# Four-layer sequence mixer on one NeuronCore: the gate tiles and the latent norm of layer 0, and the head norms of layer 3, laid out another way

## The chip, the cores and the metric

The kernel runs on one core of a Trainium2 chip. The metric is the device time of one execution in microseconds (us). The engines are named as in the profile: PE is TensorE (matmul), PEld its weight loads, DVE is VectorE, ACT is ScalarE, POOL is GpSimd, SP is SyncE.

## What is computed

The input is `x`, 256 tokens by 2048 features in fp32. Four layers follow one another: latent attention (layer 0), mLSTM (layer 1), HGRN2 (layer 2) and an attention with forget bias (layer 3). The change touches layers 0 and 3 alone. Of the reference, cut to what matters:

```python
def _mla_mixer(x, cos, sin, w_in, q_norm, w_qb, kv_norm, w_kvb, w_out):        # layer 0
    proj = x @ w_in                                                             # 512 + 512 + 64 + 2048 columns
    c_q, c_kv, k_rope, z = jnp.split(
        proj, [Q_LORA, Q_LORA + KV_LORA, Q_LORA + KV_LORA + QK_ROPE], axis=-1)
    q = (_rmsnorm(c_q, q_norm) @ w_qb).reshape(b, s, MLA_HEADS, MLA_QK)
    kv = (_rmsnorm(c_kv, kv_norm) @ w_kvb).reshape(b, s, MLA_HEADS, QK_NOPE + V_HEAD)
    ...
    attn = _chunk_causal_attention(q, k, v).reshape(b, s, MLA_WIDTH)
    return (attn * jax.nn.silu(z)) @ w_out

def head_rmsnorm(x, w):                                                         # layer 3: keys, queries, outputs
    xf = x.astype(jnp.float32)
    return xf * lax.rsqrt(jnp.mean(xf * xf, axis=-1, keepdims=True) + EPS) * w.astype(jnp.float32)
```

In layer 3 keys, queries and attention outputs are each normed per head (16 heads of 128).

## The kernel before

**The stream of products.** All projections are one stream of units through the three engines. A unit is two 128-row blocks of a weight matrix by up to 512 columns. SP loads it to `wraw` (8 buffers). ACT rounds it to fp32r (`high`, L249), DVE forms the rest `wraw - whi` (`low`, L257), and PE multiplies (`products`, L287 to L289: `x_hi*w_hi`, `x_hi*w_lo`, `x_lo*w_hi` for two row blocks and two token halves, 12 matmuls). `whi` and `wlo` have 4 buffers (`SPLIT`), so that ACT may be 4 units ahead of PE: `high` of unit n waits until PE is done with unit n-4 (`w_used`), `low` waits for `high`, and PE for `low`. A tile of the output is 16 row blocks (8 units) where the input is the layer's, 4 row blocks (2 units) where it is the latents'. `evac` copies a finished tile out of PSUM, the first token half on ACT (L329, in layer 3 L988) and the second on DVE (L335, L1596), in the step three units (`LAG`) behind its last unit.

**The order of side work.** Each engine's program is written out by hand as a loop over p, the units of a phase: first the stream's own part of unit p, then side work that hangs on certain values of p. An engine does its instructions in order, so that a side step that waits holds up the stream's next unit on that engine.

**Layer 0.** The phases are `l0_in` (tiles c_q, c_kv, and a narrow one of 64 columns for the rotary key: 24 units), `l0_0` to `l0_3`, and `l0_out` (32 units). Phase `l0_s` holds some gate tiles z (512 columns of `w_in`, 8 units each) and then four small tiles, 2 units each: queries (384 columns) and keys and values (512 columns) of two head pairs. `Z_FIRST` says which gate tiles a phase holds. Its products are followed one phase later by the attention of its four heads, in 11 stages (`l0_side`), which PE does after unit `i * nu // 11` of a phase of nu units (`spread`), and ACT and DVE three units later:

```python
        Z_FIRST = [0, 2, 3, 4, 4]
...
        def l0_at(name):
            return spread(L0_STAGES, 12 if name == "l0_out" else length(name))
```

So `l0_0` has 24 units, `l0_1` and `l0_2` 16, and `l0_3` 8. A group's stages begin with the rotation of the queries (`rope`, L1671 to L1674 on DVE) and the gate's exponentials (`z_exp`, L1045 to L1047 on ACT); then PE transposes queries and keys (`pair`, L2393 to L2396), and the scores, softmax (L562), transposes (L571), values (L587 to L589) of four heads follow; last `back` turns the group's output (L381 on PE, L394 on ACT, L409 on DVE) for `l0_out`, whose first unit waits for the third group's.

**The latent norm** stands between `l0_in` and the small tiles of `l0_0`. ACT squares the two latents for both token halves with a running sum (`latents`, four ACTIVATEs on L1017, after unit 4 of `l0_0`), DVE makes the mean (L1686), ACT takes `Ln` and `Exp` (L978, L979), DVE scales the latents (`latents2`, L1695), PE turns them (`latents2`, four groups of four transposes on L381, after unit 7), and each of the four groups then goes DVE (L403, times the weight column) to ACT (L394) to DVE (L409) to become `tb_hi` and `tb_lo` (`latents3`, all four in one piece after unit 10). The key's rotary part takes its way through PE, DVE, PE and ACT between them (L2357, L1679 to L1684, L2364, L1028).

**Layer 3.** `l3_kv` and `l3_q` have four groups of four heads, 16 units each. Three things are normed in a group: the keys at step 3 of the next `l3_kv` group (`kv_side`), the queries at step 11 of their own (`q_side` `norm`), and the outputs in step 9 of the next `l3_q` group (`post`). Each norm is this: ACT takes eight Squares with accumulator output, one for each head and token half, every one waiting for the one before (L1376 for keys and queries, L1440 for outputs); DVE scales the eight sums (L2206); ACT takes `Ln` and `Exp` (L1381, L1383); DVE multiplies (L2209, twice). DVE is in `head_norm` from the L2206 on, and ACT in `inverse_root`.

Of the kernel before, what the change touches and what calls it, by code (L numbers as in the profile page):

```python
# [84 lines left out]
def build(nc, a, out):  # L85

    with ExitStack() as ctx:
# [125 lines left out]
        Z_FIRST = [0, 2, 3, 4, 4]  # L213
# [595 lines left out]
        sqj = A(P)  # L809
# [3 lines left out]
        l3 = sems(3, "r_dg r_row f_row f_e f_ok ksq kv_ krs kn kt kT qsq qv qrs qn qt qT sc msk mx ex pt ptc pv o "  # L813
# [148 lines left out]
        def _(act):  # L962
# [37 lines left out]
            first_step("l0_in", TA, False)  # L1000
            for p in range(SPLIT, length("l0_in")):
                step(act, high, evac, "l0_in", p)
                if p == 12 + LAG:
                    act.wait_ge(rope_arg, 2)
                    nc.scalar.activation(sin.rearrange("p a b -> p (a b)"), angle[:, 4, :], ACT.Sin).then_inc(rope_ok, 1)
                    nc.scalar.activation(cos.rearrange("p a b -> p (a b)"), angle[:, 5, :], ACT.Sin).then_inc(rope_ok, 1)

                    nc.scalar.add_instruction(mybir.InstLoadActFuncSet(
                        name=nc.get_next_instruction_name(), engine=mybir.EngineType.Activation,
                        act_func_set_id=LN_EXP_SET, ins=[], outs=[]))  # L1010

# [14 lines left out]
            def latents3():  # L1026
                act.wait_ge(l0["kr_pe"], 1)
                nc.scalar.activation(krT, ps[:, 0, 0:T], ACT.Copy).then_inc(l0["kr_T"], 1)  # L1028
                for j in range(2):
                    for b in range(TB):  # L1030
                        turn_act(act, turn, TBf[0][:, 4 * j:4 * j + 4, b * P:(b + 1) * P], True)
# [337 lines left out]
            def squares(pre, src, g):  # L1369

                for b in range(TB):
# [13 lines left out]
            def kv_side(g, p):  # L1385
                def norm():
                    landed(act, "l3_kv", 0, g)
                    squares("k", qw3, g)
                    inverse_root(l3["kv_"], l3["krs"], g)
# [29 lines left out]
            def q_side(g, u):  # L1419
                c = 4 * g  # L1420

                def norm():
                    landed(act, "l3_q", 0, g)
                    squares("q", qw3, g)
# [7 lines left out]
                def post():  # L1432
# [3 lines left out]
                    for b in range(TB):  # L1436
                        for h in range(4):
                            if b or h:
                                act.wait_ge(l3["sq"], 8 * g + 4 * b + h)
                            nc.scalar.activation(sqj, o3[:, b, h * HD:(h + 1) * HD], ACT.Square,  # L1440
                                                 accum_out=sm[:, 32 + 4 * b + h:33 + 4 * b + h]).then_inc(l3["sq"], 1)
# [62 lines left out]
        def _(dve):  # L1504
# [171 lines left out]
            def latents():  # L1676
# [20 lines left out]
            def latents3():  # L1697
                for j in range(2):
                    for b in range(TB):
                        d = (slice(4 * j, 4 * j + 4), slice(b * P, (b + 1) * P))  # L1700
                        turn_dve(dve, turn, TBf[0][:, d[0], d[1]], TBf[1][:, d[0], d[1]], colA[:, 4 * j:4 * j + 4])
# [501 lines left out]
            def head_norm(dst, src, sq, vs, rs, on, g):  # L2203

                dve.wait_ge(sq, 8 * g + 8)
# [14 lines left out]
            def kv_side(g, p):  # L2220
                if p == late("l3_kv", 0):
                    head_norm(qw3, qw3, l3["ksq"], l3["kv_"], l3["krs"], l3["kn"], g)
# [20 lines left out]
            def q_side(g, u):  # L2243

                def norm():
                    head_norm(qw3, qw3, l3["qsq"], l3["qv"], l3["qrs"], l3["qn"], g)
# [12 lines left out]
                def post():  # L2259
                    head_norm(o3, o3, l3["sq"], l3["v"], l3["rs"], l3["on"], g)  # L2260
# [63 lines left out]
        def _(pe):  # L2324
# [28 lines left out]
            def key_part():  # L2353
                landed(pe, "l0_in", 2)
                pe.wait_ge(col_ok, 3)
                for b in range(TB):
# [477 lines left out]
```

## Time and profile before

| | |
|---|---|
| median of 3 runs | 1892.11 us (1891.86 to 1893.95) |
| the profiled execution | 1891.89 us |
| its span in the trace | 1890.10 us |
| PE busy, share of the span | 1856.6 us, 98% |
| DVE busy | 1241.5 us, 66% |
| ACT busy | 982.9 us, 52% |
| DMA: mean rate over the span | 169 GB/s, 319.28 MB |

The profiled execution's own time is 1.8 us above its span, which is what lies around the trace, and it lies 0.2 us below the median. A PE that is busy for 98% isn't one at its peak: the ends of matmuls are modelled (a row has 0.39 us where the next matmul starts 0.23 us after it), so that idle time in a row of PE understates the time lost by about 0.16 us each. The start of one row minus the start of the row before it gives the loss without that.

### The profile page before, as it was taken

How to read it: one execution, taken by the hardware profiler on the slowest of the kernel's cores; microseconds unless marked ns; L12 is line 12 of the kernel's file. 1: busy time of each engine (PE TensorE's matmuls, PEld its weight loads, DVE VectorE, ACT ScalarE, POOL GpSimd, SP SyncE). 2: the span in 40 equal slices, each digit the busy share in tenths (PEclk: the TensorE clock that was granted, in tenths of full speed). 3: DMA queues.
4: the chain of work that ended last, by engine and by line, in shares of the span. 5: the costliest groups of instructions: out<-in, count | busy, mean ns of one | idle time of the engine just before them, and what ended most of it. 6: DMA issues, size and time to landing. Idle time of an engine off the chain costs nothing.

```text
span 1890.1 us, 25046 instructions
## 1 busy us (share of the span) xinstructions
PE 1856.6 (98%) x9049; PEld 1559.8 (83%) x9049; DVE 1241.5 (66%) x1672; ACT 982.9 (52%) x1516; POOL 27.6 (1%) x106
## 2 busy tenths in 40 slices
PE   8999989999999999999999999999999999999999
PEld 7888878878888888887888888888878888878787
DVE  6566665687557755658777777777766555566664
ACT  4455564355456545536554454544435455566652
POOL 4000000000000000000000000000000000000000
PEclk9999999999999999999999999999999999999999
DMA  6665434468789877565545454544456566545453
GB/s 233 210 187 149 145 117 135 145 206 184 182 164 201 183 184 168 200 237 156 161 160 157 144 167 144 164 147 156 146 166 204 179 189 191 164 142 161 146 170 116
DMA packets 170207, 319.28 MB, mean 169 GB/s; under 512 B 16601, under 2 KB 20849, under 8 KB 169345
## 3 DMA queue, kind: packets, MB, share of 16 engines
q1 hardware_dynamic: 168992, 313.70, 56.7%
q10 hardware_dynamic: 576, 4.19, 0.5%
q8 instruction: 60, 0.98, 0.2%
q0 software_dynamic: 544, 0.13, 0.0%
q14 instruction: 35, 0.28, 0.0%
HBM read 315.88 MB, written 2.10 MB: 168 GB/s over the span
## 4 chain that ended last, share of the span: by engine, by line
PE 45%; DVE 2%; ACT 2%; issue 2%; ACTq 0%; DVEq 0%
PE acc L287 13%; PE acc L289 13%; PE acc L288 13%; PE ps L2640 3%; PE ps L538 1%; ACT whi L249 1%; DVE wlo L257 1%; PE ps L2624 0%; DVE arena L2014 0%; PE ps L381 0%; ACT arena L1440 0%; ACT arena L1376 0%; PE ps L2614 0%; PE ps L571 0%; PE ps L2721 0%
## 5 line engine op out<-in xcount | busy, mean ns | idle before, releaser
L257 DVE TENSOR_TENSOR wlo<-wraw,whi 128x1024 fp32r<-128x1024 f32 (+3 forms) x616 | 713.7, 1178 | 412.6 <-ACT whi L249 409.8
L249 ACT ACTIVATE whi<-wraw 128x1024 fp32r<-128x1024 f32 (+3 forms) x616 | 615.0, 1017 | 340.2 <-PE acc L289 334.4
L287 PE MATMUL acc<-whi,ta_hi 128*128 128x512 f32 x1664 | 659.4, 396 | 2.5 <-DVE wlo L257 2.3
L289 PE MATMUL acc<-whi,ta_lo 128*128 128x512 f32 x1664 | 648.6, 390 | 0.0
L288 PE MATMUL acc<-wlo,ta_hi 128*128 128x512 f32 x1664 | 647.9, 389 | 0.0
L287 PEld LDWEIGHTS acc<-whi,ta_hi 128*128 128x128 f32 x1664 | 312.6, 188 | 68.1 <-issue 3.4
L289 PEld LDWEIGHTS acc<-whi,ta_lo 128*128 128x128 f32 x1664 | 312.3, 188 | 66.6
L288 PEld LDWEIGHTS acc<-wlo,ta_hi 128*128 128x128 f32 x1664 | 312.8, 188 | 61.8
L287 PE MATMUL acc<-whi,tb_hi 128*128 128x512 f32 (+1 forms) x704 | 278.6, 396 | 8.2 <-DVE wlo L257 6.5
L289 PE MATMUL acc<-whi,tb_lo 128*128 128x512 f32 (+1 forms) x704 | 271.9, 386 | 0.0
L288 PE MATMUL acc<-wlo,tb_hi 128*128 128x512 f32 (+1 forms) x704 | 271.7, 386 | 0.0
L287 PEld LDWEIGHTS acc<-whi,tb_hi 128*128 128x128 f32 x704 | 132.7, 189 | 34.7 <-DVE wlo L257 9.1
L289 PEld LDWEIGHTS acc<-whi,tb_lo 128*128 128x128 f32 x704 | 132.7, 189 | 26.0
L288 PEld LDWEIGHTS acc<-wlo,tb_hi 128*128 128x128 f32 x704 | 132.9, 189 | 23.4
L1304 ACT ACTIVATE arena<-arena 128x512 f32<-128x512 f32 x64 | 37.4, 634 | 122.0 <-DVE arena L2034 122.0
L2640 PEld LDWEIGHTS ps<-arena 128*128 128x128 f32 x448 | 54.3, 191 | 2.1
L2640 PE MATMUL ps<-arena 128*128 128x64 f32 x448 | 53.0, 271 | 0.0
L562 ACT ACTIVATE arena<-arena,sm 128x128 f32<-128x128 f32 x64 | 28.7, 449 | 45.5 <-DVE sm L552 44.6
L329 ACT ACTIVATE arena<-acc 128x512 f32<-128x512 f32 (+3 forms) x41 | 22.5, 549 | 44.9 <-PE acc L289 42.8
L2034 DVE TENSOR_TENSOR arena<-arena 128x1024 f32<-128x1024 f32 x32 | 38.4, 1210 | 0.0
L381 PE MATMUL ps<-ident,x_res 128*128 128x128 f32 x160 | 25.8, 314 | 11.7 <-DMA x_res<-in_x 6.0
L538 PE MATMUL ps<-arena 128*128 128x128 f32 (+1 forms) x192 | 36.8, 331 | 0.0
(312 smaller groups left out, 1324.3 us busy)
## 6 DMA issues: line engine op xcount, KB each, us to landing
wraw<-in_ml_w_in SPq DMA_DIRECT2D x128, 512.0 KB, 6.1
wraw<-in_a_w_in SPq DMA_DIRECT2D x128, 512.0 KB, 4.0
wraw<-in_kv_w SPq DMA_DIRECT2D x64, 512.0 KB, 3.8
wraw<-in_b_w_in SPq DMA_DIRECT2D x64, 512.0 KB, 4.3
wraw<-in_mla_w_in SPq DMA_DIRECT2D x48, 512.0 KB, 5.3
wraw<-in_mla_w_out SPq DMA_DIRECT2D x32, 512.0 KB, 3.7
wraw<-in_ml_w_out SPq DMA_DIRECT2D x32, 512.0 KB, 4.6
wraw<-in_a_w_out SPq DMA_DIRECT2D x32, 512.0 KB, 4.4
```

The source lines that it names most:

```text
L249: nc.scalar.activation(whi[:, n % SPLIT, :, 0:w], wraw[:, n % RAW, :, 0:w], ACT.Copy).then_inc(w_high, 1)
L257: nc.vector.tensor_tensor(wlo[:, n % SPLIT, :, 0:w], wraw[:, n % RAW, :, 0:w], whi[:, n % SPLIT, :, 0:w].bitcast(F32), ALU.subtract).then_ ...
L287: nc.tensor.matmul(o, xh, wh, start=first, stop=False)
L288: nc.tensor.matmul(o, xh, wl, start=False, stop=False)
L289: m = nc.tensor.matmul(o, xl, wh, start=False, stop=end)
L329: nc.scalar.activation(dst, result(name, k, 0, dst.shape[0]), ACT.Copy).then_inc(out_b0, 1)
L381: m = nc.tensor.transpose(ps[:, c % 4, j * P:(j + 1) * P], s, ident[:])
L538: m = nc.tensor.matmul(o, x, y, start=i == 0, stop=i == len(parts) - 1)
L562: nc.scalar.activation(v, v, ACT.Exp, bias=sm[:, 2 * w + b:2 * w + b + 1], accum_out=sm[:, 4 + 2 * w + b:5 + 2 * w + b]).then_inc(self.l[" ...
L1304: nc.scalar.activation(d[:, :, c, :], d[:, :, c, :], ACT.Exp, scale=(-1.0, 1.0)[c]).then_inc(l2["ee"], 1)
L2034: nc.vector.tensor_tensor(dT[:, j % 2, :].rearrange("p (n r) -> p n r", r=2 * h), b, b[:, :, h - 1:h].to_broadcast([P, G4 // (2 * h), 2 * h]),
L2640: m = nc.tensor.matmul(ps[:, 2 + j % 2, n * 64:(n + 1) * 64], k[:, h, b * P:(b + 1) * P], qx[:, j % 2, n * 64:(n + 1) * 64], start=True, s ...
```

## The change

It has three parts.

1. `Z_FIRST` becomes `[0, 1, 2, 3, 4]`. Each of the phases `l0_0` to `l0_3` now holds one gate tile and 16 units, and the stages of each group spread over 16.
2. The latent norm begins in `l0_in`: the Squares stand after unit 20 (a narrow one) on ACT, the mean after `low` of unit 21 on DVE, `Ln` and `Exp` after unit 22 on ACT, the scaling after unit 0 of `l0_0` on DVE, PE's transposes after unit 1, and the four turned groups one by one after units 2, 3, 4 and 5 on ACT and DVE. The key's rotary part comes after them. PE's wait for all turned latents stands ahead of unit 8, the first of a small tile.
3. In layer 3 the eight accumulating Squares of a norm become one ACTIVATE of 128x1024 elements that writes the squares to two PSUM banks, and DVE sums them per head with one `tensor_reduce`, eight sums of 128 elements, ahead of its scaling.

```diff
-        Z_FIRST = [0, 2, 3, 4, 4]
+        Z_FIRST = [0, 1, 2, 3, 4]
...
+                if p == 20:
+                    latents()
+                if p == 22:
+                    latents2()
+
+            def latents3(i):
+                j, b = i // 2, i % 2
+                turn_act(act, turn, TBf[0][:, 4 * j:4 * j + 4, b * P:(b + 1) * P], True)
...
                 step(act, high, evac, "l0_0", p, 0, ("l0_in", 0))
-                if p == 4:
-                    latents()
-                if p == 6:
-                    latents2()
+                if 2 <= p < 6:
+                    latents3(p - 2)
                 if p == 10:
-                    latents3()
+                    key_part()
...
-            def squares(pre, src, g):
-
-                for b in range(TB):
-                    for h in range(4):
-                        n = 8 * g + 4 * b + h
-                        if b or h:
-                            act.wait_ge(l3[pre + "sq"], n)
-                        nc.scalar.activation(sqj, src[:, b, h * HD:(h + 1) * HD], ACT.Square,
-                                             accum_out=sm[:, 32 + 4 * b + h:33 + 4 * b + h]).then_inc(l3[pre + "sq"], 1)
+            def squares(done, src):
+
+                nc.scalar.activation(ps2(2), src.rearrange("p b n -> p (b n)"), ACT.Square).then_inc(done, 1)
...
+                if p == 21:
+                    dve.wait_ge(l0["lat_sq"], 4)
+                    nc.vector.tensor_scalar(sm[:, SMALL + 4:SMALL + 8], sm[:, SMALL:SMALL + 4], 1.0 / LORA, EPS,
+                                            ALU.mult, ALU.add).then_inc(l0["lat_v"], 1)
...
                 step(dve, low, evac, "l0_0", p, 0, ("l0_in", 0))
-                if p == 4:
-                    latents()
-                if p == 6:
+                if p == 0:
                     latents2()
-                if p == 10:
-                    latents3()
+                if 2 <= p < 6:
+                    latents3(p - 2)
+                if p == 7:
+                    key_part()
...
-            def head_norm(dst, src, sq, vs, rs, on, g):
-
-                dve.wait_ge(sq, 8 * g + 8)
+            def head_norm(dst, src, sq, ss, vs, rs, on, g):
+
+                dve.wait_ge(sq, g + 1)
+                nc.vector.tensor_reduce(sm[:, 32:40], ps2(2).rearrange("p (n d) -> p n d", d=HD), AX,
+                                        ALU.add).then_inc(ss, 1)
+                dve.wait_ge(ss, g + 1)
                 nc.vector.tensor_scalar(sm[:, 32:40], sm[:, 32:40], 1.0 / HD, EPS, ALU.mult, ALU.add).then_inc(vs, 1)
...
             for p in range(length("l0_0")):
-                if p == 16:
+                if p == 8:
                     pe.wait_ge(tr_lo, 12)
                 products(pe, "l0_0", p, lambda k, q: latent_src(k, q, 0))
                 if p == 1:
+                    latents2()
+                if p == 4:
                     key_part()
-                if p == 4:
+                if p == 8:
                     latents()
-                if p == 7:
-                    latents2()
```

**How the order moves, first place: ACT at the end of `l0_in` and in the first units of `l0_0`.** `whi<-wraw 128x2x64` is `high` of a narrow unit, `128x1024` of a wide one, `arena,sm<-arena` are the Squares of the latents, `sm<-sm` are `Ln` and `Exp`, and `tb_hi<-tmpT` are the turned groups. Before:

```order
L249 ACTIVATE whi<-wraw 128x2x64 x5
L249 ACTIVATE whi<-wraw 128x1024 x3
L329 ACTIVATE arena<-acc 64x128
L249 ACTIVATE whi<-wraw 128x1024 x2
L1017 ACTIVATE arena,sm<-arena 128x512 x4
L249 ACTIVATE whi<-wraw 128x1024 x2
L978 ACTIVATE sm<-sm 128x4
L979 ACTIVATE sm<-sm 128x4
L249 ACTIVATE whi<-wraw 128x1024 x4
L329 ACTIVATE arena<-acc 128x512
L1028 ACTIVATE arena<-ps 128x256
L394 ACTIVATE tb_hi<-tmpT 128x4x128 x4
```

With the change:

```order
L249 ACTIVATE whi<-wraw 128x2x64 x2
L1004 ACTIVATE arena,sm<-arena 128x512 x4
L249 ACTIVATE whi<-wraw 128x2x64 x2
L977 ACTIVATE sm<-sm 128x4
L978 ACTIVATE sm<-sm 128x4
L249 ACTIVATE whi<-wraw 128x2x64
L249 ACTIVATE whi<-wraw 128x1024 x3
L329 ACTIVATE arena<-acc 64x128
L394 ACTIVATE tb_hi<-tmpT 128x4x128
L249 ACTIVATE whi<-wraw 128x1024
L394 ACTIVATE tb_hi<-tmpT 128x4x128
L249 ACTIVATE whi<-wraw 128x1024
```

The Squares stand ahead of three narrow units where they stood behind five wide ones, and the turned groups, which stood in one piece, have a `high` between each two.

**Second place: DVE where the third group's attention begins** (in phase `l0_3`). The rows from L1671 are the rotation (L1666 with the change), L1717 (L1708) the gate, L1724 (L1715) the copy of the transposed keys, L257 is `low` of one unit. Before:

```order
L1671 TENSOR_TENSOR arena<-arena 128x128 x4
L1673 TENSOR_TENSOR arena<-arena 128x4x32
L1674 TENSOR_TENSOR arena<-arena 128x4x32
L1717 TENSOR_TENSOR arena<-arena 128x1024
L1724 COPY arena<-ps 128x512
L257 TENSOR_TENSOR wlo<-wraw,whi 128x2x384
L335 COPY arena<-acc 128x384
L547 SCALAR_TENSOR_TENSOR arena<-ps,mask 128x384
```

With the change:

```order
L1666 TENSOR_TENSOR arena<-arena 128x128 x4
L1668 TENSOR_TENSOR arena<-arena 128x4x32
L1669 TENSOR_TENSOR arena<-arena 128x4x32
L1708 TENSOR_TENSOR arena<-arena 128x1024
L257 TENSOR_TENSOR wlo<-wraw,whi 128x1024
L1715 COPY arena<-ps 128x512
L257 TENSOR_TENSOR wlo<-wraw,whi 128x1024
L547 SCALAR_TENSOR_TENSOR arena<-ps,mask 128x384
```

A unit of the stream lies between the rotation and what follows PE's transposes, where none lay: this group now has the order that the first two had.

## Rows read from the trace of the kernel before

**Rows 1.** The page's part 1: busy us (share of the span) x instructions.

```profile
PE 1856.6 (98%) x9049; PEld 1559.8 (83%) x9049; DVE 1241.5 (66%) x1672; ACT 982.9 (52%) x1516; POOL 27.6 (1%) x106
```

**Rows 2.** Waits of PE: engine, line, waited for: us in total, times, longest.

```profile
PE acc L287 <- DVE wlo L257: 8.8, 12, 1.6
...
PE ps L587 <- ACT arena L579: 2.3, 2, 1.7
PE ps L2393 <- DVE arena L1674: 2.2, 1, 2.2
...
PE acc L287 <- DVE ta_lo L409: 1.7, 1, 1.7
...
PE ps L381 <- issue: 1.1, 1, 1.1
```

**Rows 3.** Stretches: us, busy PE, PEld, DVE, ACT, POOL, granted clock, DMA, GB/s.

```profile
63.69:130.96 67.27, 66.07 (x309) 55.34 (x309) 41.64 (x53) 32.45 (x46) 0.00 (x0) 1.00 0.67 211
130.96:184.59 53.63, 53.63 (x289) 47.11 (x288) 34.79 (x62) 30.09 (x52) 0.00 (x0) 1.00 0.51 150
...
238.22:278.59 40.37, 34.18 (x194) 30.61 (x192) 26.45 (x55) 23.46 (x46) 0.00 (x0) 0.96 0.38 118
...
244.00:247.00 3.00, 3.00 (x11) 3.00 (x11) 1.82 (x3) 2.08 (x4) 0.00 (x0) 0.50 0.09 35
384.00:391.00 7.00, 6.43 (x30) 6.03 (x31) 5.47 (x11) 5.32 (x15) 0.00 (x0) 0.52 0.30 71
```

**Rows 4.** Timeline of ACT, end of l0_in: start, us, instruction [idle before <-releaser].

```profile
58.25 0.57 ACT L249 ACTIVATE whi<-wraw 128x128 fp32r<-128x128 f32 x2
...
59.87 0.31 ACT L249 ACTIVATE whi<-wraw 128x128 fp32r<-128x128 f32 x1 [0.37 <-PE acc L277]
...
67.76 0.61 ACT L1017 ACTIVATE arena<-arena 128x512 f32<-128x512 f32 x1
...
70.22 1.04 ACT L249 ACTIVATE whi<-wraw 128x1024 fp32r<-128x1024 f32 x1
```

**Rows 5.** Timeline of DVE, one turned group of the latents in l0_0.

```profile
88.26 0.69 DVE L403 TENSOR_TENSOR tmpT<-ps,colA 128x512 f32<-128x512 f32 x1 [0.93 <-PE ps L381]
89.65 0.69 DVE L409 TENSOR_TENSOR tb_lo<-tmpT,tb_hi 128x512 fp32r<-128x512 f32 x1 [0.70 <-ACT tb_hi L394]
```

**Rows 6.** Timeline of ACT in the second l3_q group: both norms.

```profile
1651.77 0.31 ACT L1440 ACTIVATE arena<-arena 128x128 f32<-128x128 f32 x1 [2.93 <-DVE arena L2251]
...
1655.82 1.04 ACT L249 ACTIVATE whi<-wraw 128x1024 fp32r<-128x1024 f32 x1
...
1660.39 0.31 ACT L1376 ACTIVATE arena<-arena 128x128 f32<-128x128 f32 x1 [2.00 <-DVE arena L1596]
...
1664.42 1.04 ACT L249 ACTIVATE whi<-wraw 128x1024 fp32r<-128x1024 f32 x1
```

**Rows 7.** Timeline of DVE in the same stretch.

```profile
1663.87 0.17 DVE L2206 TENSOR_SCALAR sm<-sm 128x8 f32<-128x8 f32 x1 [2.44 <-ACT arena L1376]
...
1665.76 1.22 DVE L257 TENSOR_TENSOR wlo<-wraw,whi 128x1024 fp32r<-128x1024 f32 x1
```

**Rows 8.** Timeline of PE in the same stretch.

```profile
1664.80 0.39 PE L288 MATMUL acc<-wlo,tb_hi 128*128 128x512 f32 x1
1665.03 0.39 PE L289 MATMUL acc<-whi,tb_lo 128*128 128x512 f32 x1
...
1667.04 0.50 PE L287 MATMUL acc<-whi,tb_hi 128*128 128x512 f32 x1 [1.62 <-DVE wlo L257]
...
1671.20 0.50 PE L287 MATMUL acc<-whi,tb_hi 128*128 128x512 f32 x1 [0.19 <-DVE wlo L257]
```

**Rows 9.** Duration ns of reductions and a 128x1024 ACTIVATE from PSUM: min/median/max.

```profile
L551 DVE TENSOR_REDUCE sm<-arena x32: 285/286/288, 142.4 to 1805.7; 128x1 f32<-128x128 f32 x32
...
L552 DVE TENSOR_REDUCE sm<-arena x32: 407/409/411, 142.6 to 1805.9; 128x1 f32<-128x256 f32 x32
...
L1429 ACT ACTIVATE arena<-ps,sm x4: 1096/1099/1116, 1615.9 to 1783.0; 128x1024 f32<-128x1024 f32 x4
```

More of the change, by code:

```diff
@@ L808, in build @@
         rdiag = kT3[:, 13, :]
[L809 to L813 removed]
+        l3 = sems(3, "r_dg r_row f_row f_e f_ok kss qss oss ksq kv_ krs kn kt kT qsq qv qrs qn qt qT sc msk mx ex pt ptc pv o "
                      "ge gs sq v rs on og ogp tmp hi lo")
@@ L997, in ln_rstd @@
                 nc.scalar.activation(nrm[:, b, 2:3], nrm[:, b, 1:2], ACT.Exp, scale=-0.5).then_inc(nrm_a, 1)
[L1000 to L1010, printed above, removed]
             def latents():
@@ L1024, in latents2, with key_part @@
                      sm[:, SMALL + 12:SMALL + 16]).then_inc(l0["lat_r"], 1)
-            def latents3():
+            first_step("l0_in", TA, False)
+            for p in range(SPLIT, length("l0_in")):
+                step(act, high, evac, "l0_in", p)
+                if p == 12 + LAG:
+                    act.wait_ge(rope_arg, 2)
+                    nc.scalar.activation(sin.rearrange("p a b -> p (a b)"), angle[:, 4, :], ACT.Sin).then_inc(rope_ok, 1)
+                    nc.scalar.activation(cos.rearrange("p a b -> p (a b)"), angle[:, 5, :], ACT.Sin).then_inc(rope_ok, 1)
+                    nc.scalar.add_instruction(mybir.InstLoadActFuncSet(
+                        name=nc.get_next_instruction_name(), engine=mybir.EngineType.Activation,
+                        act_func_set_id=LN_EXP_SET, ins=[], outs=[]))
+                if p == 20:
[5 more added lines that the diff above has]
+                turn_act(act, turn, TBf[0][:, 4 * j:4 * j + 4, b * P:(b + 1) * P], True)
+            def key_part():
                 act.wait_ge(l0["kr_pe"], 1)
                 nc.scalar.activation(krT, ps[:, 0, 0:T], ACT.Copy).then_inc(l0["kr_T"], 1)
-                for j in range(2):
-                    for b in range(TB):
-                        turn_act(act, turn, TBf[0][:, 4 * j:4 * j + 4, b * P:(b + 1) * P], True)
             def ln_params(layer):
@@ L1387, in norm @@
                     landed(act, "l3_kv", 0, g)
-                    squares("k", qw3, g)
+                    squares(l3["ksq"], qw3)
                     inverse_root(l3["kv_"], l3["krs"], g)
@@ L1423, in norm @@
                     landed(act, "l3_q", 0, g)
-                    squares("q", qw3, g)
+                    squares(l3["qsq"], qw3)
                     inverse_root(l3["qv"], l3["qrs"], g)
@@ L1435, in post @@
                     act.wait_ge(l3["qn"], 2 * g + 2)
[L1436 to L1441, printed above, removed]
+                    squares(l3["sq"], o3)
                     inverse_root(l3["v"], l3["rs"], g)
@@ L1674, in rotate, with key_part @@
                 nc.vector.tensor_tensor(dst[..., 32:64], t[2], t[3], ALU.add).then_inc(*n)
-            def latents():
+            def key_part():
                 dve.wait_ge(l0["kr_in"], 1)
@@ L1695, in latents2, with latents3 @@
                         nc.vector.tensor_scalar(v, v, sm[:, i:i + 1], None, ALU.mult).then_inc(l0["lat_ok"], 1)
[L1697 to L1701, printed above, removed]
+            def latents3(i):
+                j, b = i // 2, i % 2
+                d = (slice(4 * j, 4 * j + 4), slice(b * P, (b + 1) * P))
+                turn_dve(dve, turn, TBf[0][:, d[0], d[1]], TBf[1][:, d[0], d[1]], colA[:, 4 * j:4 * j + 4])
             def l0_side(s, p, at):
@@ L2221, in kv_side @@
                 if p == late("l3_kv", 0):
-                    head_norm(qw3, qw3, l3["ksq"], l3["kv_"], l3["krs"], l3["kn"], g)
+                    head_norm(qw3, qw3, l3["ksq"], l3["kss"], l3["kv_"], l3["krs"], l3["kn"], g)
             for p in range(6, length("l3_f")):
@@ L2245, in norm @@
                 def norm():
-                    head_norm(qw3, qw3, l3["qsq"], l3["qv"], l3["qrs"], l3["qn"], g)
+                    head_norm(qw3, qw3, l3["qsq"], l3["qss"], l3["qv"], l3["qrs"], l3["qn"], g)
                 def out_(hh):
@@ L2259, in post @@
                 def post():
-                    head_norm(o3, o3, l3["sq"], l3["v"], l3["rs"], l3["on"], g)
+                    head_norm(o3, o3, l3["sq"], l3["oss"], l3["v"], l3["rs"], l3["on"], g)
                     dve.wait_ge(l3["on"], 2 * g + 2)
@@ L2355, in key_part @@
                 pe.wait_ge(col_ok, 3)
+                pe.wait_ge(tr_lo, turn.n - 3)
                 for b in range(TB):
```

5 lines of the change are left out of this document (removed).

## The prediction

> **What bounds the kernel now.** I read the page's part 1 first: PE is busy for 98% of the span, DVE for 66%, ACT for 52% [rows 1]. So PE sets the end, and the change gives PE no work and takes none away: the same matmuls stand in another order. All that it can move is time in which PE stands still or runs slowly. For that I read PE's waits. The reader is to see that they are few and short, and which belong to the changed places [rows 2]: 2.2 us ahead of the transposes of a pair (L2393, one time), 2.3 us ahead of the values (L587, two times), 1.7 us ahead of the first unit of `l0_out` (released by L409, one time), 1.1 us ahead of the turned latents (L381 <- issue), and 8.8 us in twelve waits for `low`. Then I read the stretches [rows 3], cut at the first matmul of each phase: `l0_0` takes 67.27 us, `l0_1` 53.63 us and so does `l0_2` (its row reads alike), `l0_3` 40.37 us. In the 53.63 us PE is busy throughout, in the 40.37 us for 34.18. The granted clock of that last stretch is 0.96, and it is the lower of the two levels (0.50, 1.2 GHz) from 244 to 247 us. PE stood still for 2.2 us just before. The other such stretch, 384 to 391 us, stands behind a long wait too and is not touched by the change.
>
> **Part 1, one gate tile per phase.** `l0_3` grows to the shape of `l0_1` and `l0_2`: one gate tile, four small ones, the same eleven stages over 16 units. I take their time for it, 53.63 us: +13.26 us against 40.37. `l0_0` loses one gate tile. A unit is 12 matmuls that start 0.227 us apart (0.23 in the two rows ahead of the stall) [rows 8], 2.72 us, and a tile 8 units: -21.76 us. The difference of the two, -8.5 us, is work that isn't less: it is the waits of `l0_3` that go. I check it by the waits: 2.2 + 2.3 + 1.7 us are 6.2 us, for each of four about 0.16 us more than the idle time says (matmul rows are 0.39 us long and start 0.23 us apart), and 3.4 us or so at half clock give back 1.7 us: 8.5 us. The two ways agree. What hides `rope`, `z_exp` and the copies in the new `l0_3` is the wide unit that now lies between them, 2.72 us, as in the phases before. The wait of `l0_out` for the third group goes too: `back` now stands behind unit 14, with unit 15 between it and `l0_out`, where it stood behind the last. What is late next: nothing in `l0_1` to `l0_3`; `l0_out` has its own 12-unit spread, and it is unchanged.
>
> **Part 2, the latent norm.** Removed: the wait ahead of the turned latents, 1.1 us idle, 1.25 us from start to start [rows 2]. Added are waits in two places, since the four Squares now stand ahead of three narrow units and the turns ahead of wide ones.
> First, `l0_in`. A narrow unit takes PE 0.68 us (ACT's `high` is 0.31 us long and waits 0.37 us for it) [rows 4]. The `high` of units 19 and 20 start at 58.25 us, so that the Squares can start at 58.8; four of them hold ACT for 2.46 us (67.76 to 70.22) [rows 4], to 61.3. Unit 21 reaches PE after `high` and `low`, 0.3 us each, at 62.05; PE wanted it at 61.0. Then `Ln` and `Exp` (0.2 us each, and a hop through DVE before them) hold up unit 23's `high` and with it unit 0 of `l0_0`: 1.0 us more, where 0.6 us of waiting stood before. Net the first wide unit starts 1.4 us later.
> Second, `l0_0`. Behind `low` of each of units 2 to 5 DVE makes a product for ACT, ACT rounds it, and only then may ACT do its next `high`. One turn is 1.39 us from L403 to L409 [rows 5]. The loop high, low, L403, L394 takes, start to start, 1.09 + 1.14 + 0.72 + 0.56 = 3.51 us, where PE needs 2.72. PE's own 1.7 us of transposes cover the first round; units 4, 5 and 6 come 0.8 us late each, less 0.3 us for the key's transposes: 2.1 us.
> The DVE's scaling (four operations) lies ahead of unit 1's `low` and ends as PE ends unit 0: nothing. The key's part lies beside PE's small tiles: nothing; were that cover gone, it would cost its 2 us on DVE.
> Layer 0 together: +13.26 - 21.76 - 1.25 + 1.4 + 2.1 = **-6.3 us**.
>
> **Part 3, single Squares.** In each of three `l3_q` groups the outputs' norm and the queries' meet three units apart. A norm holds ACT from its first Square to its next `high` for 4.05 us (1651.77 to 1655.82) and again for 4.03 us (1660.39 to 1664.42) [rows 6]; the chain ends in `low` at 1665.76 [rows 7] and unit 12 at 1667.04, 2.01 us after the matmul before it: 1.78 us lost; the next unit loses 0.19 + 0.16 us [rows 8]. That is 2.1 us in each of three groups, most of the 8.8 us of [rows 2]. Now the Square of 128x1024 takes 1.05 to 1.10 us (the nearest ACTIVATE of that size reads PSUM and takes 1.10) [rows 9], and the sum is a reduction. No row has one of this size or from PSUM. 128 elements take 0.286 us and 256 take 0.409 [rows 9]: 0.96 ns an element, so 1024 take 1.15 us. The lower bound is 0.41 us (one of 256), the upper eight of 128 in a row, 2.3 us; I take 1.15, since the slope has fitted both rows. Square, reduction and hops then stand for 2.25 us where 3.5 us stood ahead of L2206 (1660.39 to 1663.87) [rows 6, 7]. Each norm is 1.2 us shorter; two in a chain give unit 12's `low` at 1663.4, done 0.6 us ahead of need, and unit 13 just in time. So all of it goes: 3 x 2.1 = **-6.4 us**. The key norms and the last group's output norm have no wait behind them; they give nothing.
> The Trainium skill ("VectorE: DVE Perf Modes", rules for kernel authors) speaks against this part: it has `tensor_reduce` as the slowest DVE operation, at one element a cycle, and its table gives an operand in PSUM a larger fixed cost, 62 cycles or an estimated 0.065 us. By it unit 13 would be about 0.13 us late in each group, and the sum 0.4 us smaller.
>
> **The sum.** 1891.89 - 6.3 - 6.4 = 1879.2 us for the profiled execution; the median lies 0.2 us above it, so **1879.4 us**, 0.7% faster.
>
> **The rivals.**
> *The latents eat the gain.* The loop of 3.51 us may be longer, since on each hop one engine waits for the other, and a longer one costs four times; were it 4.2 us, layer 0 would lose some 3 us more, and if the clock falls once in the broken narrow units, 1.7 us on top. Against it: every hop is read from rows. Layer 0 then gives 1.6 us, and the time is 1884.
> *DVE becomes what layer 3 waits for.* If the reduction takes the upper bound, 2.3 us, the norm is as long as before, and part 3 gives nothing: 1885.8 us. Against it: it is one instruction, and a row of eight pays eight starts.
> *`l0_3`'s wait moves.* The first group of stages in `l0_out` has a 12-unit spread and may now meet an ACT that is behind by the third group's end: the 2.2 us and the 1.7 us of low clock return, 1883.3 us. For it: DVE still has rotation and gate in one piece. Against it: before, the same `l0_out` came after a crowded `l0_3` and lost nothing behind its first unit.
> *Slower: the clock stays low through `l0_0`.* The new waits lie close together, at 61, 64, 79, 82 and 85 us. If PE falls to 1.2 GHz and stays there over the eight wide units, each takes 5.44 us: +21.8 us, less the 2.1 us of waits that a slow PE no longer has: 1899 us. It decides from 5 units at the low level on (12.7 / 2.72). Against it: in this trace idle times of 1.74 and 1.69 us in `l0_3` and `l0_out` left the clock alone, and 2.2 us brought one short stretch [rows 2, 3].
> The skill ("TensorE: Matmul & The Clock Gate", what's actually happening) has the low level as the default and activity as what releases it, which is the rule by which this rival would come; the stretch of 244 to 247 us agrees in kind.
> *It doesn't do what it says*: the order of instructions shows it does, so that this has no chance of its own.
>
> **How the numbers follow.** Forecast 0.66, latents eat the gain 0.14, layer 3 gives nothing 0.06, wait moves 0.08, slower 0.03, the rest (0.03) a time between 1888 and 1896. The forecast's own range is 1876 to 1882: the reduction's price and the loop's by some tenths, and one stretch of low clock more or less at the end of layer 0, 1.7 to 3.4 us. For eight in ten I reach to the first and third rivals: 1875 to 1886. A measurement of this kernel tells from no change what is over 0.2%, 3.8 us: faster below 1888.3. That holds the forecast and three rivals, 0.94; within 0.2% 0.03; slower 0.03.
>
> **What would show it.** Right: in the profile after, `l0_1`, `l0_2` and `l0_3` take 53.6 us each, L2393, L587 and `low` <- L409 are gone from PE's waits, there is no stretch of low clock near 244 us; `l0_0` takes some 46 us, with waits of PE for `low` of 0.5 to 0.8 us at three units; in each `l3_q` group PE waits for `low` no more, the Square takes 1.1 us and the reduction 1.15. Wrong: a reduction of 2 us; PE's clock under 1.00 between 58 and 110 us; waits of over 1 us at units 4 to 6; a wait in `l0_out` that wasn't there. A time above 1888 would say that the waits of the old profile only came back in other places.

## The result and the profile after

| | median, us | lowest to highest, us | ratio to before, 95% interval |
|---|---|---|---|
| before | 1892.76 | 1891.86 to 1893.95 (4 runs) | |
| changed | 1878.16 | 1877.52 to 1878.73 (4 runs) | 0.9925 [0.9911, 0.9939] |
| changed, measured again | 1878.17 | 1877.92 to 1878.59 (5 runs; before 1892.30) | 0.9925 [0.9911, 0.9938] |

The changed kernel is 0.75% faster, 14.6 us in the first measurement and 14.1 us in the second. The forecast was 1879.4 us in a range of 1875 to 1886. The span of the profiled execution fell by 14.3 us, from 1890.1 to 1875.8.

Part 1 of the page, as in [rows 1]:

```profile
PE 1853.0 (99%) x9049; PEld 1558.7 (83%) x9049; DVE 1255.0 (67%) x1684; ACT 955.7 (51%) x1336; POOL 27.4 (1%) x106
```

PE does the same 9049 matmuls. ACT lost 180 instructions (the Squares of layer 3, and the reads of their sums), DVE has twelve more. Of the 14.3 us only 3.6 us are in PE's busy time; the rest was idle.

The waits of PE (engine, line, what it waited for: us in total, times, the longest), against [rows 2]:

```profile
PE acc L287 <- DVE wlo L257: 4.6, 9, 1.1
PE ps L381 <- DVE x_res L1621: 3.6, 1, 3.6
...
PE acc L275 <- DVE ta_lo L478: 0.8, 1, 0.8
PE acc L275 <- DVE wlo L257: 0.7, 1, 0.7
```

The four lines that the forecast said would go are gone: the transposes of a pair, L587, `ta_lo` L409, and L381 <- issue. What waits for `low` fell from 8.8 to 4.6 us (6.1 us in a second profile of the changed kernel, where the waits near 12 and 18 us, at the start of `l0_in`, are longer), and a wait of 0.7 us at a narrow unit is new. The wait of 3.6 us at the start of layer 1 was there before.

The stretches, cut at the first matmul of each phase as in [rows 3] (length; busy us of PE, PEld, DVE, ACT, POOL; granted clock; DMA share; GB/s):

```profile
64.69:110.14 45.45, 44.53 (x212) 37.35 (x213) 30.89 (x43) 20.51 (x27) 0.00 (x0) 1.00 0.67 213
110.14:163.77 53.63, 53.63 (x289) 47.12 (x288) 34.78 (x62) 30.09 (x52) 0.00 (x0) 1.00 0.51 149
...
217.40:271.03 53.63, 53.63 (x289) 47.12 (x288) 35.05 (x63) 30.09 (x52) 0.00 (x0) 1.00 0.49 153
243.00:250.00 7.00, 7.00 (x47) 6.64 (x46) 4.57 (x8) 2.90 (x5) 0.00 (x0) 1.00 0.45 139
376.90:383.70 6.80, 6.00 (x29) 5.60 (x29) 4.80 (x11) 5.34 (x13) 0.00 (x0) 0.50 0.41 104
```

`l0_3` (217.40 to 271.03) now takes to the hundredth what `l0_1` and `l0_2` take, with PE busy throughout. `l0_0` went from 67.27 to 45.45 us. Near 244 us the clock is full; the stretch at half clock at the start of layer 1, which follows the wait of 3.6 us, is where it was relative to its work. From the tiny transposes at 38 us, which the change doesn't touch, to the start of `l0_out` it is 7.3 us less than before: +13.26 (`l0_3`) - 21.82 (`l0_0`) + 1.22 (a later start of unit 0).

**The end of `l0_in`.** ACT, against [rows 4] (start, length, engine, line, operation, in brackets the idle time before it and what ended it):

```profile
58.51 0.62 ACT L1004 ACTIVATE arena<-arena 128x512 f32<-128x512 f32 x1
...
60.96 0.49 ACT L249 ACTIVATE whi<-wraw 128x128 fp32r<-128x128 f32 x2
61.69 0.20 ACT L977 ACTIVATE sm<-sm 128x4 f32<-128x4 f32 x1 [0.24 <-DVE sm L1657]
...
62.04 3.14 ACT L249 ACTIVATE whi<-wraw 128x128 fp32r<-128x128 f32 x4
```

The four Squares hold ACT for 2.45 us (58.51 to 60.96), as in the old place, and `Ln` and `Exp` follow 0.73 us later. PE sees both holes, and then three more in the loop of the turned groups:

```profile
61.64 0.33 PE L275 MATMUL acc<-ta_hi,whi 128*64 128x256 f32 x1 [0.72 <-DVE wlo L257]
64.69 0.47 PE L287 MATMUL acc<-whi,ta_hi 128*128 128x512 f32 x1 [0.77 <-DVE wlo L257]
78.00 0.50 PE L287 MATMUL acc<-whi,ta_hi 128*128 128x512 f32 x1 [0.35 <-DVE wlo L257]
78.34 0.40 PE L288 MATMUL acc<-wlo,ta_hi 128*128 128x512 f32 x1
...
81.48 0.50 PE L287 MATMUL acc<-whi,ta_hi 128*128 128x512 f32 x1 [0.15 <-DVE wlo L257]
84.95 0.50 PE L287 MATMUL acc<-whi,ta_hi 128*128 128x512 f32 x1 [0.42 <-DVE wlo L257]
```

Units 4, 5 and 6 start 3.48 and 3.47 us apart where a unit takes 2.72. That is the pace of the loop. First ACT, then DVE:

```profile
75.64 1.04 ACT L249 ACTIVATE whi<-wraw 128x1024 fp32r<-128x1024 f32 x1
78.58 0.63 ACT L394 ACTIVATE tb_hi<-tmpT 128x512 fp32r<-128x512 f32 x1 [1.89 <-DVE tmpT L403]
79.12 1.04 ACT L249 ACTIVATE whi<-wraw 128x1024 fp32r<-128x1024 f32 x1
```

```profile
76.72 1.23 DVE L257 TENSOR_TENSOR wlo<-wraw,whi 128x1024 fp32r<-128x1024 f32 x1 [0.26 <-ACT whi L249]
77.87 0.68 DVE L403 TENSOR_TENSOR tmpT<-ps,colA 128x512 f32<-128x512 f32 x1
79.25 0.69 DVE L409 TENSOR_TENSOR tb_lo<-tmpT,tb_hi 128x512 fp32r<-128x512 f32 x1 [0.70 <-ACT tb_hi L394]
```

From `high` to `high` it is 3.48 us (75.64 to 79.12): `high` 1.08, `low` 1.15, L403 0.71, L394 0.54, each counted to the start of the next. Each engine waits for the other once a turn (1.89 us on ACT, 0.26 and 0.70 us on DVE), so that neither is busy all the time and both are late.

**One group of `l3_q`.** ACT and DVE, against [rows 6] and [rows 7]:

```profile
1644.36 1.03 ACT L1373 ACTIVATE ps<-arena 128x1024 f32<-128x1024 f32 x1 [2.93 <-DVE arena L2245]
1646.89 0.21 ACT L1377 ACTIVATE sm<-sm 128x8 f32<-128x8 f32 x1 [1.50 <-DVE sm L2200]
...
1647.24 1.05 ACT L249 ACTIVATE whi<-wraw 128x1024 fp32r<-128x1024 f32 x1
...
1651.81 1.03 ACT L1373 ACTIVATE ps<-arena 128x1024 f32<-128x1024 f32 x1 [2.00 <-DVE arena L1587]
...
1654.69 1.04 ACT L249 ACTIVATE whi<-wraw 128x1024 fp32r<-128x1024 f32 x1
```

```profile
1645.42 1.23 DVE L2197 TENSOR_REDUCE sm<-ps 128x8 f32<-128x1024 f32 x1 [1.18 <-ACT ps L1373]
1646.68 0.17 DVE L2200 TENSOR_SCALAR sm<-sm 128x8 f32<-128x8 f32 x1
...
1652.87 1.22 DVE L2197 TENSOR_REDUCE sm<-ps 128x8 f32<-128x1024 f32 x1
...
1656.03 1.22 DVE L257 TENSOR_TENSOR wlo<-wraw,whi 128x1024 fp32r<-128x1024 f32 x1
```

Each norm holds ACT for 2.88 us (1644.36 to 1647.24, and 1651.81 to 1654.69) instead of 4.05 and 4.03. `low` of unit 12, which came at 1665.76 and made PE wait 1.62 us [rows 7, 8], now comes in time: PE has no wait in any `l3_q`. One group follows the other after 53.34 us (the reduction at 1645.42 and at 1698.76), where it was 55.65 us before (the wait at 1667.04 and at 1722.69). That is 2.3 us in each of three groups, 6.9 us in all. With the 7.3 us of layer 0 this is 14.2 of the 14.3 us. What is left over is small and nearly cancels: PE is 0.2 us ahead at 38 us already, and layers 1 and 2 take 0.3 us more (PE's wait of 1.09 us ends near 1383 us, 999.25 us after its wait of 3.6 us ended, where it was 998.98 us).

### The profile page after: what moved, and what is told of

The parts are those of the page before. It is cut to its first block, busy times and chain, and to the rows that moved or that the text cites. A ratio compares the mean times of both kernels' runs of the same rounds, so it can differ in the third digit from the quotient of the medians.

```text
span 1875.8 us, 24810 instructions
## 1 busy us (share of the span) xinstructions
PE 1853.0 (99%) x9049; PEld 1558.7 (83%) x9049; DVE 1255.0 (67%) x1684; ACT 955.7 (51%) x1336; POOL 27.4 (1%) x106
## 4 chain that ended last, share of the span: by engine, by line
PE 48%; DVE 1%; issue 1%; ACT 1%; DVEq 0%; ACTq 0%
PE acc L287 14%; PE acc L289 14%; PE acc L288 14%; PE ps L2634 3%; PE ps L538 1%; PE ps L2618 0%; DVE arena L2005 0%; PE ps L2715 0%; PE ps L381 0%; PE ps L2608 0%; ACT whi L249 0%; PE ps L571 0%; ACT arena L1294 0%; DVE arena L1994 0%; DVE arena L1995 0%
## 5 line engine op out<-in xcount | busy, mean ns | idle before, releaser
L257 DVE TENSOR_TENSOR wlo<-wraw,whi 128x1024 fp32r<-128x1024 f32 (+3 forms) x616 | 713.8, 1177 | 414.5 <-ACT whi L249 411.6
L381 PE MATMUL ps<-ident,x_res 128*128 128x128 f32 x160 | 25.3, 310 | 11.7 <-DMA x_res<-in_x 5.9
```

Of the source, the lines that this page charges most:

```text
L257: nc.vector.tensor_tensor(wlo[:, n % SPLIT, :, 0:w], wraw[:, n % RAW, :, 0:w], whi[:, n % SPLIT, :, 0:w].bitcast(F32), ALU.subtract).then_ ...
L381: m = nc.tensor.transpose(ps[:, c % 4, j * P:(j + 1) * P], s, ident[:])
```

## The experiments

Theory: the two parts of layer 0 give some 7 us together, and the Squares 6 to 7 us, each by the waits of PE that they end. Rivals: one part of layer 0 alone does it; the reduction is free or is the bound; stretches of low clock explain what the waits don't. "Before" was run anew beside each of the three groups of experiments (medians 1892.29, 1892.30 and 1892.20).

### Each part alone

**Part 3 alone** (the kernel before with one Square for each norm, and the reduction):

```diff
-                nc.scalar.activation(sqj, src[:, b, h * HD:(h + 1) * HD], ACT.Square,
-                                     accum_out=sm[:, 32 + 4 * b + h:33 + 4 * b + h]).then_inc(l3[pre + "sq"], 1)
+                nc.scalar.activation(ps2(2), src.rearrange("p b n -> p (b n)"), ACT.Square).then_inc(done, 1)
...
+                nc.vector.tensor_reduce(sm[:, 32:40], ps2(2).rearrange("p (n d) -> p n d", d=HD), AX,
+                                        ALU.add).then_inc(ss, 1)
```

> The kernel before with part 3 alone: one Square of 128x1024 into PSUM and one reduction on DVE in place of eight accumulating Squares. Theory (each norm holds ACT and the stream behind it 1.2 us less, and three l3_q groups stop waiting): the l3_q groups take 53.3 us instead of 55.65, PE's waits for low at units 12 and 13 are gone, layer 0 is as before; 6.9 us faster, 1885.9 us, ratio 0.9964. Rival (the gain of the change came from layer 0 alone, and DVE, with one operation more, only takes over the wait): ratio 1.000.

Measured: 1886.78 us (1884.95 to 1886.99), ratio 0.9964 [0.9950, 0.9978]. PE's waits for `low` fell from 8.8 to 3.9 us; all waits of layer 0 stood as before.

**Parts 1 and 2 without part 3** (the changed kernel with the old Squares, the diff above reversed):

> The changed kernel with the old eight Squares in layer 3, so parts 1 and 2 alone. Theory (the parts don't touch each other): l0_1 to l0_3 at 53.63 us each, no low clock near 240 us, l0_0 at 45.5 us, l3_q groups back at 55.65 us; 7.4 us faster than before, 1885.4 us, ratio 0.9961. Rival (the stretch of low clock in layer 0 was chance, and stands in other runs of either kernel): the gain is 5.7 us, ratio 0.997.

Measured: 1885.65 us (1885.20 to 1886.09), ratio 0.9961 [0.9947, 0.9975]. All old waits of layer 0 are gone, those for `low` are 10.5 us in fifteen: the old twelve and the new ones. The two halves give 5.5 and 6.6 us, 12.1 in all; the whole gives 14.1 us. The intervals of some 2.7 us for each half can't say whether the 2.0 us between them are real, but the traces can. Up to the end of PE's wait of 3.6 us at the start of layer 1, the kernel without part 3 is 7.7 us ahead of the kernel before (376.31 for 384.01 us), as the whole change is (376.33). From the wait that ends near 1383 us to the end of the span, part 3 alone takes 500.2 us and so does the whole change, for 507.1 before. That is 14.6 us for the two. What the halves lack lies between, in layers 1 and 2, which no part touches: there each half's profile takes 1000.4 us, for 999.0 and 999.3 in the kernel before and the changed one, with a stretch of low clock (near 866 us in part 3 alone, near 858 in the other) that these two don't have. So the parts add up, and the 2 us are no interaction of layer 0 with layer 3.

**Part 1 alone**, the latents left in their old place. The first tile that needs them now stands behind 8 units, so PE's wait moves with it:

```diff
-        Z_FIRST = [0, 2, 3, 4, 4]
+        Z_FIRST = [0, 1, 2, 3, 4]
...
-                if p == 16:
+                if p == 8:
                     pe.wait_ge(tr_lo, 12)
```

> The kernel before with part 1 alone: one gate tile per phase, the latent norm where it was (PE's wait for the turned latents stands ahead of unit 8, since the small tiles begin there). Theory (part 1 gains 8.5 us in l0_3 but takes the cover of one gate tile from the latents' turns): PE waits some 7 us ahead of unit 8 of l0_0, from the transposes to the last low part, and perhaps falls to the low clock behind that wait (1.7 to 3.4 us more); 1891.3 us without a fall, 1893 to 1895 with one. Rival (the even gates alone make the gain of layer 0, and the latent norm was moved for nothing): 1885.4 us, ratio 0.996.

Measured: 1892.68 us (1891.67 to 1893.58, 10 runs), ratio 0.9999 [0.9990, 1.0009]. The wait of PE, and the stretch around it:

```profile
PE acc L287 <- DVE tb_lo L409: 6.8, 1, 6.8
```

```profile
93.20:100.00 6.80, 3.61 (x11) 3.61 (x12) 3.21 (x4) 2.00 (x3) 0.00 (x0) 0.51 0.15 26
```

PE stands still for 6.8 us until 96.39, and the clock is at its low level from 93 to 100 us, over 3.6 us of work, which at the full clock would be about 1.8 us. The 6.8 and the 1.8 us pay back what `l0_3` gives (8.5 us).

**Part 2 alone**, the old gates:

```diff
+                if p == 20:
+                    latents()
+                if p == 22:
+                    latents2()
...
+                if 2 <= p < 6:
+                    latents3(p - 2)
```

> The kernel before with part 2 alone: the latent norm begun in l0_in and turned step by step, the gate tiles as before (two in l0_0). Theory (the new waits of 0.9, 0.9, 0.5, 0.3 and 0.6 us, 3.2 us in all, stand against 2.2 us of old ones): 1.0 us slower than before, 1893.8 us, ratio 1.0005, with the waits of l0_3 and the stretch of low clock there as before. Rival (starting the norm early is a gain of its own, since PE no longer waits ahead of the turned latents): 1.3 us faster, 1891.5 us.

Measured: 1892.99 us (1891.32 to 1894.20, 10 runs), ratio 1.0001 [0.9991, 1.0011]. The new waits of `l0_in` and `l0_0` stand at their places, and those of `l0_3` as well. The expected 1893.8 and its rival's 1891.5 can't be told apart by the time. The trace surprised in one point. PE waits 2.19 us until 244.15, as before, but the clock doesn't fall:

```profile
244.00:247.00 3.00, 2.85 (x20) 2.85 (x21) 1.92 (x3) 2.07 (x5) 0.00 (x0) 1.00 0.47 171
```

So neither part of layer 0 gives anything that can be measured, and the two together give 6.6 us. Part 1 needs the latents by unit 8, and only part 2 brings them there. Part 2 alone costs 1.2 us: from the tiny transposes at 38 us to the rotary transposes of the next phase PE takes 99.54 us, for 98.37 before.

### The price of the reduction

The changed kernel once more, with a second reduction of the same data ahead of the first:

```diff
+                nc.vector.tensor_reduce(sm[:, 40:48], ps2(2).rearrange("p (n d) -> p n d", d=HD), AX, ALU.add)
                 nc.vector.tensor_reduce(sm[:, 32:40], ps2(2).rearrange("p (n d) -> p n d", d=HD), AX,
                                         ALU.add).then_inc(ss, 1)
```

> The changed kernel once more, as the measure for the three runs beside it: 1878.2 us, ratio 0.9925.

> The changed kernel with the reduction of each of the twelve norms done twice (the first into a place that is written over). Theory (in the three groups where two norms meet, DVE's operations are links of the chain to the stream's next unit, which has 0.5 us to spare): the chain grows by 2.4 us, PE waits 1.9 us ahead of unit 12 and some tenths ahead of unit 13 again; 5.7 to 7 us over the changed kernel, 1884.5 us. Rival (DVE is busy for 67% and has room, a reduction more is hidden): 1878.2 us, no wait of PE in l3_q.

Measured: the changed kernel 1878.17 us, as above; with two reductions 1884.45 us (1884.12 to 1885.63), ratio 0.9960 [0.9944, 0.9975]. DVE and PE in one group:

```profile
1653.89 1.23 DVE L2197 TENSOR_REDUCE sm<-ps 128x8 f32<-128x1024 f32 x1
1655.04 1.22 DVE L2198 TENSOR_REDUCE sm<-ps 128x8 f32<-128x1024 f32 x1
...
1658.19 1.22 DVE L257 TENSOR_TENSOR wlo<-wraw,whi 128x1024 fp32r<-128x1024 f32 x1
```

```profile
1659.46 0.50 PE L287 MATMUL acc<-whi,tb_hi 128*128 128x512 f32 x1 [1.59 <-DVE wlo L257]
1663.63 0.50 PE L287 MATMUL acc<-whi,tb_hi 128*128 128x512 f32 x1 [0.20 <-DVE wlo L257]
```

With 2.37 us in place of 1.23 us the old waits are back, 1.59 and 0.20 us where 1.62 and 0.19 stood [rows 8], and 6.3 us are lost. DVE is 67% busy in the whole kernel and still bounds this place. The rival "DVE becomes what layer 3 waits for" had its mechanism right, and only its price (2.3 us) wasn't met.

### The waits that the change brought

**The four turned groups in one piece, behind unit 5**, on ACT and DVE:

```diff
-                if 2 <= p < 6:
-                    latents3(p - 2)
+                if p == 5:
+                    for i in range(4):
+                        latents3(i)
```

> The changed kernel with the four turned groups of the latents in one piece after unit 5 of l0_0 on ACT and DVE, where they stand one by one after units 2 to 5. Theory (what costs is the loop high, low, product, rounding, 3.5 us a unit against 2.72 of PE, while one piece of 8 us is bridged by the four units that are ready ahead of it): the waits of 0.5, 0.3 and 0.6 us ahead of units 4 to 6 go, one of at most 0.3 us comes; 1.1 us faster than the changed kernel, 1877.1 us. Rival (one piece holds ACT for three units, and PE runs dry ahead of unit 6 or 8): 1 to 3 us slower.

Measured: 1876.41 us (1876.02 to 1877.49), ratio 0.9918 [0.9904, 0.9931], 1.8 us less than the changed kernel. PE's waits at units 4 to 6 are gone and only the two of the norm are left:

```profile
61.31 0.33 PE L275 MATMUL acc<-ta_hi,whi 128*64 128x256 f32 x1 [0.72 <-DVE wlo L257]
64.36 0.47 PE L287 MATMUL acc<-whi,ta_hi 128*128 128x512 f32 x1 [0.78 <-DVE wlo L257]
```

ACT shows why, first in the changed kernel and then with the groups in one piece:

```profile
71.63 0.63 ACT L394 ACTIVATE tb_hi<-tmpT 128x512 fp32r<-128x512 f32 x1 [6.29 <-DVE tmpT L403]
72.17 1.05 ACT L249 ACTIVATE whi<-wraw 128x1024 fp32r<-128x1024 f32 x1
```

```profile
64.91 1.05 ACT L249 ACTIVATE whi<-wraw 128x1024 fp32r<-128x1024 f32 x1
...
75.11 0.63 ACT L394 ACTIVATE tb_hi<-tmpT 128x512 fp32r<-128x512 f32 x1 [1.36 <-DVE tmpT L403]
```

ACT and DVE don't overlap in one piece either: in each group ACT waits 1.36 us (1.89 in the first) and DVE 0.70 us, a group takes 1.99 us, and the four hold the stream for 7.2 us. What differs is what goes ahead of them. In the changed kernel the first group stands behind unit 2 and waits there for PE's transposes; ACT is idle for 6.29 us, and `high` of unit 3 starts only at 72.17. Behind unit 5 it starts at 64.91, and `high` of unit 6 at 79.64 instead of 82.59. The expected reason holds: PE lives on the units that are ready. But this version moved the groups to a later place and joined them at once, and no run tells the one from the other.

**The Squares behind unit 1 of `l0_0` too**, not in `l0_in`, and the turned groups in one piece behind unit 7 (here ACT's part; DVE's and PE's moved with it):

```diff
-                if p == 20:
-                    latents()
-                if p == 22:
-                    latents2()
...
-                if 2 <= p < 6:
-                    latents3(p - 2)
+                if p == 1:
+                    latents()
+                if p == 3:
+                    latents2()
+                if p == 7:
+                    for i in range(4):
+                        latents3(i)
```

> The changed kernel with the latent norm begun in l0_0: Squares after unit 1, mean after unit 2, Ln and Exp after unit 3, scaling after unit 4, PE's transposes after unit 3, and all four turned groups in one piece after unit 7. Theory (the Squares cost where the units are narrow, 0.68 us each of PE, and nothing among wide ones; the eight wide units are cover enough): the waits ahead of narrow unit 21 and of unit 0 shrink from 0.9 and 0.9 us to one of 0.7 us, and those ahead of units 4 to 6 are gone; 2.3 us faster than the changed kernel, 1875.9 us. Rival (with one gate tile the chain is too long for eight units, so that it had to begin in l0_in): PE waits ahead of unit 8, 1 to 4 us slower than the changed kernel.

Measured: 1875.62 us (1875.27 to 1875.95), ratio 0.9911 [0.9897, 0.9924]. It is the fastest of all, 16.7 us below the kernel before and 2.5 us below the changed one. The version before it had given 1.8 of the 2.5 us. From the tiny transposes at 38 us to the rotary transposes of the next phase PE takes 77.77 us in the changed kernel, 76.04 with the groups in one piece and 74.81 here. PE has one wait left in this region, 0.52 us, which the kernel before had as well:

```profile
63.70 0.47 PE L287 MATMUL acc<-whi,ta_hi 128*128 128x512 f32 x1 [0.52 <-DVE wlo L257]
```

So the norm did not have to begin in the first projection. Four Squares are hidden behind wide units of 2.72 us, and not behind narrow ones of 0.68 us.

### Whose the low clock is

Part 2 alone left a question: the kernel before had a stretch of low clock behind its 2.2 us wait, and this kernel none behind the same wait. Some profiles also showed one near 866 us (layer 1 to 2) that the kernel before didn't have. Four more single profiled executions, with no edit: the kernel before twice, part 2 alone and part 3 alone once each.

> The kernel before once more, to see whether its 3.4 us stretch at half clock behind the 2.2 us wait (244 to 247 us) belongs to the kernel or to the execution. If to the kernel: a granted clock of 0.50 from 244 to 247 us again, 1.00 from 864 to 868 us, and a span of 1890.1 us within 0.5 us. If to the execution: one or both of the two places read the other way, and the span moves by 1.7 us for each.

> The same as the look before it, a second time: a stretch that belongs to the kernel is there in every look, one that belongs to the execution in some of them.

> Part 2 alone, which had the 2.2 us wait and no low clock behind it. If that belongs to the kernel: 1.00 at 244 to 247 us again. If to the execution: 0.50 there is as likely, and the span is then 1.7 us more than 1891.6 for this stretch, less 1.7 us where the one near 866 us stays away.

> Part 3 alone, whose work up to layer 3 is that of the kernel before. If stretches of low clock belong to the kernel: 0.50 near 245 and near 866 us again, span 1885.0. If to the execution: one of them may be missing, and the span is 1883.3 us with one stretch, 1881.6 with none.

Measured: 1892.45, 1892.28, 1893.24 and 1886.67 us. Two stretches of each of the two new profiles of the kernel before, the first one first:

```profile
244.00:247.00 3.00, 3.00 (x22) 3.00 (x23) 1.83 (x2) 2.08 (x5) 0.00 (x0) 1.00 0.48 170
865.00:867.00 2.00, 2.00 (x6) 1.54 (x6) 1.29 (x2) 1.68 (x3) 0.00 (x0) 0.53 0.93 330
```

```profile
244.00:247.00 3.00, 3.00 (x14) 3.00 (x12) 1.82 (x3) 2.08 (x4) 0.00 (x0) 0.56 0.24 94
865.00:867.00 2.00, 2.00 (x11) 1.65 (x10) 2.00 (x3) 1.97 (x6) 0.00 (x0) 1.00 0.64 143
```

The first has no low clock near 244 us and has it near 866; the second the other way round. Part 2 alone, which had none near 244 us, has one there now (0.69 over the same 3 us) and none near 866; part 3 alone has both, as the first time. So a stretch belongs to the execution and not to the kernel. What decides it in one execution is open.

## Why the prediction was right, point by point

**What bounds the kernel.** Right: PE does the same work, and all 14.3 us are time in which it stood still or ran slowly.

**Part 1.** `l0_3` was to take 53.63 us and did. Its waits went, and none came up in `l0_out`, so the rival of the moved wait fell. The check by the waits (6.2 + 0.6 + 1.7 = 8.5 us) was less sound than it seemed. Its last 1.7 us came from a stretch of low clock that another execution of the same kernel doesn't have. It was right against the profiled execution, where the stretch happened to stand, and that much of the agreement is luck; for the medians it counts by its frequency, five of seven profiles with the 2.2 us wait.

**Part 2.** The start of the first wide unit moved by 1.22 us for a forecast of 1.4. `l0_0` took 45.45 us, and the terms made 67.27 - 21.76 - 1.25 + 2.1 = 46.4 us. The term that was too large is the 2.1 us of waits at units 4 to 6. The loop was right (3.48 for 3.51 us), but the three waits cost 1.7 us, by the traces of the changed kernel and of the version with the turned groups in one piece: from the tiny transposes at 38 us to the rotary transposes of the next phase it is 77.77 us in the one and 76.04 in the other. And the old profile had lost time here that no wait named, behind its own turned groups (`low` of unit 11 starts only at 96.57 us):

```profile
97.35 0.39 PE L289 MATMUL acc<-whi,ta_lo 128*128 128x512 f32 x1
97.85 0.50 PE L287 MATMUL acc<-whi,ta_hi 128*128 128x512 f32 x1
98.19 0.40 PE L288 MATMUL acc<-wlo,ta_hi 128*128 128x512 f32 x1
```

These start 0.50 and 0.34 us apart instead of 0.227, a loss of 0.38 us that left with the change. I had read the list of waits there and not the starts. Layer 0 gave 7.3 us for a forecast of 6.3. That the latents eat the gain fell with it: 1.2 + 1.7 us were all that they cost.

**Part 3.** The Square took 1.03 us (forecast 1.05 to 1.10), the reduction 1.22 us (1.15), the norm on ACT is shorter by 1.17 us (1.2), and three groups gave 6.9 us (6.4). The difference is 0.2 us a group, 0.1 for each of its two waits. PE's matmul behind a wait is followed by the next only 0.34 us later, not 0.227, as in the rows at 78.00 and 78.34; I had counted the gap ahead of the wait's end and not this.
One sentence of the forecast was wrong: that no row has a reduction of this size. Layer 2 of the kernel before has four, by the view of the line L2083 (length lowest/median/highest in ns, first and last start, shape):

```profile
L2083 DVE TENSOR_REDUCE sm<-arena x4: 1220/1220/1220, 994.8 to 1320.7; 128x8 f32<-128x1024 f32 x4
```

and the new lines of the changed kernel, the Square and the reduction, read:

```profile
L1373 ACT ACTIVATE ps<-arena x12: 1017/1029/1031, 1439.7 to 1804.3; 128x1024 f32<-128x1024 f32 x12
...
L2197 DVE TENSOR_REDUCE sm<-ps x12: 1217/1223/1225, 1440.9 to 1805.4; 128x8 f32<-128x1024 f32 x12
```

The row would have given 1.22 us at once, with no slope from 128 and 256 elements and no upper bound of 2.3 us. That the slope fitted both rows said nothing, since a line goes through any two. It was 6% low, and the rival's chance of 0.06 would have been near nothing.
The Trainium skill ("VectorE: DVE Perf Modes", the TRN2 errata) gives an operand in PSUM a larger fixed cost, 120 cycles for 58, an estimated 0.065 us more here. The traces don't agree for this operation: 1.223 us from PSUM, 1.220 us from SBUF. Nor was unit 13 late.

**The slower case.** The clock stayed at 1.00 from 58 to 110.14 us through five waits of 0.15 to 0.77 us. Its condition, waits close together in running wide units, was met in part, and nothing fell. It is in part 1 alone, where PE stood still for 6.8 us, that the clock fell in `l0_0`.

**The sum.** The forecast was right in its mechanism and 1.6 us too small against the profile (12.7 for 14.3 us): 1.0 us in layer 0 and 0.5 us in layer 3, by the terms above, all on the same side.

## What to carry to other kernels

Find the row of the same shape in the whole trace before estimating one from a slope, and read the starts of the bounding engine's rows besides its waits. A gain that rests on two moves can look worthless when each is tried alone, as here (1892.7 and 1893.0 us alone, 1885.7 together), so follow which wait takes the place of the one removed. Where side work must go into a stream that two engines feed in turn, don't place it ahead of the work that feeds the next units while it still waits for something; here, behind unit 5 and in one piece, it cost PE nothing. Side work that is long beside a narrow unit belongs among wide ones.

## What the runs showed of the hardware

A stretch of half clock 3.4 us long, behind a wait of 2.2 us (near 244 us) or behind waits of 1.6 and 0.5 us (near 866 us), comes in some executions of one and the same kernel and not in others. Near 244 us it came in five of the seven profiles with that wait, near 866 us in six of all fourteen. The one of 6.8 us behind the wait of 3.6 us came in all fourteen. The Trainium skill ("TensorE: Matmul & The Clock Gate", what's actually happening) has the low level as the default and activity as what releases it. That agrees in kind, since each stretch stands behind idle time, but no run shows why equal idle time brings it once and not again.

DVE's reduction of 128x1024 to 128x8 takes the time of its elementwise operation of that size (1.22 us both), and as long from PSUM as from SBUF.
